# Expert loop: the down projection as three products of rounded halves, the second block's inner tile rounded later, both output copies on ScalarE

## What is computed

```
def moe_ffn(h, w_router, router_bias, w_e_gate, w_e_up, w_e_down, w_sh_gate, w_sh_up, w_sh_down):
    ...
    def expert_block(args):
        tok_b, w_b, e = args
        xb = h[tok_b]
        hid = jax.nn.silu(xb @ w_e_gate[e]) * (xb @ w_e_up[e])
        return (hid @ w_e_down[e]) * w_b[:, None].astype(h.dtype)
    out = lax.map(expert_block, (buf_tok.reshape(n_blocks, MOE_BLOCK), buf_w.reshape(n_blocks, MOE_BLOCK), block_e))
    routed = jax.ops.segment_sum(out.reshape(n_pad, d), buf_tok, num_segments=n_tok)
```

## Time and profile before

| | us |
|---|---|
| median of 3 runs | 3445.34 (3444.95 to 3451.27) |
| the profiled execution's own time | 3434.75 |
| its span, first to last instruction | 3432.9 |
| first product of the expert loop to the last (L2081 to L2096) | 987.3 to 1664.6 |

### The profile page before, as it was taken

One profiled execution on the slowest core, in us unless ns is written; L12 is line 12 of the kernel. 1 busy time (PEld: TensorE's weight loads), 2 busy tenths in 40 slices (PEclk: granted clock), 3 DMA queues, 4 the chain that ended last, 5 costly groups with the idle time before them and its releaser, 6 DMA issues.

```text
span 3432.9 us, 44220 instructions
## 1 busy us (share of the span) xinstructions
PE 3263.4 (95%) x16966; PEld 2567.5 (75%) x16966; DVE 1600.3 (47%) x2236; ACT 1448.6 (42%) x1847; POOL 1313.7 (38%) x1068
## 2 busy tenths in 40 slices
PE   7999998999889999999879999998999998899999
PEld 4788876778556666666567888887888877688887
DVE  4555437355476666666444554546221232452121
ACT  4344445612335555555444555555322242342221
POOL 2322136444123333333235434433444443354444
PEclk9999999999899999999989999999999999999999
DMA  5212110255259999999833222231322211022222
GB/s 212 68 50 62 38 50 13 87 184 196 76 219 344 349 344 357 377 366 367 311 108 104 89 84 83 81 101 60 110 99 90 99 58 62 25 98 98 98 98 74
DMA packets 98530, 496.85 MB, mean 145 GB/s; under 512 B 22446, under 2 KB 22702, under 8 KB 49728
## 3 DMA queue, kind: packets, MB, share of 16 engines
q1 hardware_dynamic: 78480, 454.86, 37.2%
q0 software_dynamic: 19888, 39.73, 3.2%
HBM read 472.48 MB, written 40.89 MB: 150 GB/s over the span
## 4 chain that ended last, share of the span: by engine, by line
PE 82%; DVE 5%; ACT 4%; DMA 3%; issue 3%; POOL 2%; SPq 0%; ACTq 0%; DVEq 0%; POOLq 0%
PE ps L283 13%; PE ps L285 13%; PE ps L284 13%; PE ps L2096 7%; PE ps L289 4%; PE ps L291 3%; PE ps L290 3%; PE ps L2081 3%; PE ps L2085 3%; PE ps L2084 3%; DMA arena<-we_gu 3%; PE ps L2634 1%; PE ps L2622 1%; PE ps L713 1%; PE ps L2070 1%
## 5 line engine op out<-in xcount | busy, mean ns | idle before, releaser
L283 PE MATMUL ps<-arena_r,arena_r 128*128 128x512 f32 x2080 | 823.9, 396 | 16.2 <-POOL ring_r L273 7.1
L284 PE MATMUL ps<-arena_r,arena_r 128*128 128x512 f32 x2080 | 813.0, 391 | 0.0
L273 POOL TENSOR_TENSOR ring_r<-ring,arena_r 128x512 fp32r<-128x512 f32 x400 | 553.0, 1413 | 644.4 <-ACT arena_r L268 644.4
L268 ACT ACTIVATE arena_r<-ring 128x2048 fp32r<-128x2048 f32 x166 | 316.8, 1910 | 407.2 <-PE ps L285 330.5
L273 POOL TENSOR_TENSOR arena_r<-ring,arena_r 128x512 fp32r<-128x512 f32 x264 | 335.1, 1301 | 381.1 <-ACT arena_r L268 381.1
L283 PEld LDWEIGHTS ps<-arena_r,arena_r 128*128 128x128 f32 x2080 | 392.6, 189 | 106.7 <-issue 18.1
L284 PEld LDWEIGHTS ps<-arena_r,arena_r 128*128 128x128 f32 x2080 | 392.8, 189 | 81.7 <-issue 1.9
L285 PE MATMUL ps<-arena_r,arena_r 128*128 128x512 f32 x1056 | 410.8, 389 | 0.0
L285 PE MATMUL ps<-arena_r,ring_r 128*128 128x512 f32 x1024 | 402.2, 393 | 0.0
L2184 DVE TENSOR_TENSOR arena_r<-arena,arena_r 128x2048 fp32r<-128x2048 f32 x132 | 301.8, 2288 | 166.1 <-ACT arena_r L2142 165.8
L2142 ACT ACTIVATE arena_r<-arena 128x2048 fp32r<-128x2048 f32 x132 | 250.9, 1910 | 125.5 <-DMA arena<-we_gu 102.7
(11 more groups left out here) (435 smaller groups left out, 5872.2 us busy)
## 6 DMA issues: line engine op xcount, KB each, us to landing
ring<-wstream SPq DMA_DIRECT2D x177, 1024.0 KB, 5.0
arena<-we_gu SPq DMA_DIRECT2D x132, 1024.0 KB, 8.0
arena<-we_down SPq DMA_DIRECT2D x66, 1024.0 KB, 7.3
arena<-arena SPq DMA_DIRECT2D x256, 64.0 KB, 2.0
arena<-ys SPq DMA_DIRECT2D x32, 512.0 KB, 7.1
arena<-wstream SPq DMA_DIRECT2D x24, 512.0 KB, 6.9
arena<-x_t SPq DMA_DIRECT2D x2, 2048.0 KB, 11.9
rope<-wstream SPq DMA_DIRECT2D x8, 512.0 KB, 8.5
```

The costliest lines, as they stand in the source:

```text
L268: act.activation(whalf(c, 0), ring[:, c % NSLOT, :], ACT.Copy).then_inc(sem("chunk_hi"), 1)
L273: ins = pool.tensor_tensor(whalf(c, 1)[:, q:q + 512], ring[:, c % NSLOT, q:q + 512], whalf(c, 0)[:, q:q + 512].bitcast(F32), ALU.subtract)
L283: pe.matmul(out, hi, rhs[0], start=start, stop=False)
L284: pe.matmul(out, hi, rhs[1], start=False, stop=False)
```

## The change

The down projection takes three products of rounded halves instead of one float32 product. For that, ScalarE gets a rounding of each block's down weights (`high_down`) and VectorE the subtraction (`low_down`), the turned inner tile of each block gets a high half by ScalarE (`hidden_high`) and a low half by VectorE (`hidden_low`) where before it had one copy, by ScalarE for block 0 and by VectorE for block 1. The new work for block 1 stands on ScalarE behind `turned(1)`, and on VectorE too. The copy of `YO[1]` goes from VectorE to ScalarE, and `high(1,1)` stands behind it. The load of `dmask_flat` is issued after the last pair, since the high half of block 1's down weights now uses its place.

```diff
             def down(s, j, first_done=None):
                 for k in range(2):
-                    mm = pe.matmul(bank(2 * s + j), HIDT[s][:, k * P:k * P + P], expert_raw(s, 2)[:, k * D + j * 512:k * D + j * 512 + 512],
-                                   start=(k == 0), stop=(k == 1))
+                    hidden = [half[:, k * P:k * P + P] for half in HIDT[s]]
+                    hi, lo = (w[:, k * D + j * 512:k * D + j * 512 + 512] for w in (expert_hi(s, 2), expert_lo(s, 2)))
+                    mm = pe.matmul(bank(2 * s + j), hidden[0], hi, start=(k == 0), stop=False)
...
+                    pe.matmul(bank(2 * s + j), hidden[0], lo, start=False, stop=False)
+                    mm = pe.matmul(bank(2 * s + j), hidden[1], hi, start=False, stop=(k == 1))
...
             def down_ready(i, s, back):
                 pe.wait_ge(sem(f"moe_hidt{s}"), i + (1 - back))
-                pe.wait_ge(sem(f"moe_w{s}2"), i * 16 + (16 - 16 * back))
+                pe.wait_ge(sem("moe_d_lo"), i * 2 + (s + 3 - 2 * back))
...
+            def high_down(s, i, back):
+                act.wait_ge(sem(f"moe_w{s}2"), i * 16 + (16 - 16 * back))
+                act.activation(expert_hi(s, 2), expert_raw(s, 2), ACT.Copy).then_inc(sem("moe_d_hi"), 1)
+
+            def hidden_high(s, i, back):
+                act.wait_ge(sem("moe_hturn"), i * 2 + (3 + s - 2 * back))
+                act.activation(HIDT[s][0], bank(6 + s, 256), ACT.Copy).then_inc(sem("moe_hidt_hi"), 1)
...
                 silu(i, 0, back)
+                high_down(0, i, back)
                 if not back:
                     turned(0, i + 2)
                     high(0, 0, i * 16 + 32)
                 silu(i, 1, back)
-                act.wait_ge(sem("moe_hturn"), i * 2 + (3 - 2 * back))
-                act.activation(HIDT[0], bank(6, 256), ACT.Copy).then_inc(sem("moe_hidt0"), 1)
+                hidden_high(0, i, back)
                 if not back:
                     turned(1, i + 2)
+                high_down(1, i, back)
+                hidden_high(1, i, back)
+                if not back:
                     high(0, 1, i * 16 + 32)
...
                 if not back:
-                    for j in range(2):
-                        high(1, j, i * 16 + 32)
+                    high(1, 0, i * 16 + 32)
+                act.wait_ge(sem("moe_d_used"), i * 2 + (4 - 2 * back))
+                act.wait_ge(sem("moe_out1"), i * 16 + (16 - 16 * back))
+                act.activation(YO[1], pf[:, 1024:2048], ACT.Copy).then_inc(sem("moe_y1"), 1)
+                act.activation(small[:, 61:62], epst[:, :], ACT.Copy).then_inc(sem("moe_y_full1"), 1)
+                if not back:
+                    high(1, 1, i * 16 + 32)
...
+            def low_down(s, i, back):
+                dve.wait_ge(sem("moe_d_hi"), i * 2 + (s + 3 - 2 * back))
+                dve.tensor_tensor(expert_lo(s, 2), expert_raw(s, 2), expert_hi(s, 2).bitcast(F32),
+                                  ALU.subtract).then_inc(sem("moe_d_lo"), 1)
+
+            def hidden_low(s, i, back):
+                dve.wait_ge(sem("moe_hidt_hi"), i * 2 + (s + 3 - 2 * back))
+                dve.tensor_tensor(HIDT[s][1], bank(6 + s, 256), HIDT[s][0].bitcast(F32),
+                                  ALU.subtract).then_inc(sem(f"moe_hidt{s}"), 1)
...
                 value(i, 0, back)
+                low_down(0, i, back)
                 if not back:
                     turned(0, i + 2)
                     low(0, 0, i * 4 + 5)
                 value(i, 1, back)
+                hidden_low(0, i, back)
                 if not back:
                     turned(1, i + 2)
-                dve.wait_ge(sem("moe_hturn"), i * 2 + (4 - 2 * back))
-                dve.tensor_copy(HIDT[1], bank(7, 256)).then_inc(sem("moe_hidt1"), 1)
+                low_down(1, i, back)
+                hidden_low(1, i, back)
                 if not back:
                     low(0, 1, i * 4 + 6)
                     low(1, 0, i * 4 + 7)
-                dve.wait_ge(sem("moe_d_used"), i * 2 + (4 - 2 * back))
-                dve.wait_ge(sem("moe_out1"), i * 16 + (16 - 16 * back))
-                dve.tensor_copy(YO[1], pf[:, 1024:2048]).then_inc(sem("moe_y1"), 1)
-                dve.tensor_copy(small[:, 61:62], epst[:, :]).then_inc(sem("moe_y_full1"), 1)
-                if not back:
                     low(1, 1, i * 4 + 8)
...
             pool.dma_start(rope[:, :, :], rope_t[1]).then_inc(sem("dil_loaded"), 16)
-            pool.dma_start(dmask_flat, dmask_t[:, 0:4 * TA]).then_inc(sem("dil_loaded"), 16)
             pool.dma_start(dmask_turned, dmask_t[:, 4 * TA:5 * TA]).then_inc(sem("dil_loaded"), 16)
             pool.dma_start(WZ, w_z).then_inc(sem("dil_loaded"), 16)
             pair_of_blocks(n - 1, False)
+            pool.dma_start(dmask_flat, dmask_t[:, 0:4 * TA]).then_inc(sem("dil_loaded"), 16)
```

More of the change, by code:

```diff
@@ L120 @@
                                        "moe_hidt", "moe_y", "moe_y_full") for s in "01") + (
-    "moe_gu_hi", "moe_gu_lo", "moe_gu_used", "moe_d_used", "moe_hturn", "moe_x_col", "moe_y_col")
+    "moe_gu_hi", "moe_gu_lo", "moe_gu_used", "moe_d_used", "moe_hturn", "moe_x_col", "moe_y_col",
+    "moe_d_hi", "moe_d_lo", "moe_hidt_hi")
 TAIL_SEMS = ("moe_left", "tl_act", "tl_weights", "tl_ranked", "tl_diag", "tl_turn", "tl_x", "tl_sq", "tl_xw", "tl_sum",
@@ L1742, in two_blocks @@
         XBT = [[rounded(4096 + 2048 * part + 1024 * s, D) for part in range(2)] for s in range(2)]
-        HIDT = [view(R + 30720 + 256 * s, 256) for s in range(2)]
+        HIDT = [[rounded(R + 30720 + 512 * s + 256 * part, 256) for part in range(2)] for s in range(2)]
         K0 = R + 31744
@@ L2167, in pair_of_blocks @@
                 if not back:
-                    for j in range(2):
-                        high(1, j, i * 16 + 32)
+                    high(1, 0, i * 16 + 32)
[5 more added lines that the diff above has]
+                    high(1, 1, i * 16 + 32)
             act.sem_inc(sem("moe_y0"), 1)
+            act.sem_inc(sem("moe_y1"), 1)
+            act.sem_inc(sem("moe_d_hi"), 2)
+            act.sem_inc(sem("moe_hidt_hi"), 2)
             for s in range(2):
@@ L2208, in pair_of_blocks @@
                     low(1, 0, i * 4 + 7)
-                dve.wait_ge(sem("moe_d_used"), i * 2 + (4 - 2 * back))
-                dve.wait_ge(sem("moe_out1"), i * 16 + (16 - 16 * back))
-                dve.tensor_copy(YO[1], pf[:, 1024:2048]).then_inc(sem("moe_y1"), 1)
-                dve.tensor_copy(small[:, 61:62], epst[:, :]).then_inc(sem("moe_y_full1"), 1)
-                if not back:
                     low(1, 1, i * 4 + 8)
-            dve.sem_inc(sem("moe_y1"), 1)
             dve.sem_inc(sem("moe_gu_lo"), 4)
+            dve.sem_inc(sem("moe_d_lo"), 2)
             for s in range(2):
```

## The result

| | before | after |
|---|---|---|
| median | 3445.14 us | 3522.3 us (3519.64 to 3525.92, 4 runs) |
| profiled execution, its span | 3434.75, 3432.9 | 3521.39, 3519.6 |
| mean granted clock | 0.979 | 0.968 |

What follows compares the result with a forecast made beforehand. TensorE looked like the bound, transfers close behind. 32 pairs at +1.24 us (+39.7), last pair -0.9 and the moved `dmask_flat` load 0.3 gave +39 on 3445.34: 3484 us, range 3467 to 3502.

Steps and rivals of the forecast that it cites:

- The chain: Expert loop, from `turned(1)` through `high_down(1)`, `low_down(1)`, `hidden_low(1)` to block 1's down products: pair becomes 21.65 us; 74%.
- TensorE's saving: Down products at 0.227 us each: 6.88 us a pair falls to 5.46, 1.42 us less if nobody waits.
- Copy of `YO[1]` free: Copy on ScalarE with `high(1,1)` behind: ready 5.5 to 6 us into the next pair, wanted 9 us in; no cost.
- I take most of it as gone, 0.1 us left per pair: Lateness of gate/up weights in the expert loop mostly vanishes in the longer pair: 0.1 us left, mean pair 21.75.
- the mean DMA share: Transfers in the expert loop, 19.5 us a pair: busy 0.90 of a 21.65 us pair instead of 0.95.
- The spare time: A late `high(0,0)` has 0.21 us to spare, then delays the pair one for one; 0.25 us before the change.
- The rival that kept the lateness: Lateness of weights in the loop stays or grows: +51, or +60 with another 0.3 us per pair, 3496 to 3505 us; 10%.
- The clock: Rival: clock drops to 1.2 GHz for the last 12 products of every pair, +79 us on top, 3563 us; 4%.
- one gap of 1.65 us that kept full clock: Evidence against the falling clock: from 2900 to 2920 TensorE is busy 16.82 of 20 us and keeps 2.4 GHz.
- a gap of 2.1 us ahead of `down(0,0)`: TensorE waits about 2.1 us in each pair as `down(0,0)` moves from 1516.16 to about 1518.30.
- The sum: 32 x 1.24 = +39.7 us for the loop's pairs, with the smaller terms +39 (bounds +35 and +53): median 3484 us.
- the last pair: Last pair of the expert loop, without next tokens to turn or such a chain: between -1.4 and 0, taken as -0.9 us.

Runs made afterwards that it cites:

- experiment 1: Changed kernel with the loop's scatters and gathers moving 64 of 1024 columns; pairs of 21.60 to 21.67 us, only the loop comparable.
- experiment 8: Changed kernel with block 1's down tile rounded before `silu(1)`, subtracted before `value(1)`, and tile (0,0) handled later; 3431.39 us.
- experiment 9: Changed kernel with block 1's down tile prepared early, `high(0,0)` directly behind `high_down(1)` and `hidden_low(0)` ahead of `value(1)`; 3429.12 us.
- experiment 6: Tile (0,0) rounded and subtracted later, behind the hidden tiles, in both kernels: 3430.16 us in the kernel before, 3512.97 us in the changed one.
- experiment 3: Changed kernel with the copy of `YO[1]` back on VectorE, behind `low(1,0)`; 3523.93 us.
- experiment 7: Useless products filling TensorE's idle time: 3518.85 us on the changed kernel, 3473.11 us on the changed kernel with tile (0,0) handled later.

## Why the prediction was wrong

- **The chain**: right. 21.65 forecast, 21.63 measured with nothing else in the way (experiment 1), each step of a short pair within 0.11 us, and experiment 8 removes it by order alone.
- **TensorE's saving**: right per product (one every 0.227 us). Of the 1.42 us a pair little was ever seen: the short pairs of experiment 9 are 0.2 us under those of experiment 6 in the kernel before, and TensorE still idles in them (busy 469.65 of 500 us).
- **Copy of `YO[1]` free**: right (experiment 3).
- **"I take most of it as gone, 0.1 us left per pair"**: this step failed. It was argued from the mean DMA share, which fell even further than the 0.90 forecast, to 0.85. What counts is when three loads in a row are asked for, and that is tied to the pair's end, not to its length. L was 10.80 before (by rows; 10.40 from the real start of the first product) and 10.66 after, so the longer pair did not bring the mean load in sooner. The spare time is as forecast (lengthening sets in at L = 10.0), but lateness now costs 0.91 us a pair, 29 us, instead of 0.1. The L of the kernel before, put into the formula of the changed one, give 0.44; the rest comes of the wider spread (8.63 to 12.85 after, 9.55 to 11.55 before). The rival that kept the lateness had 10%, and its 0.44 to 0.74 us a pair was too low as well.
- **The clock**: the rival was priced at 79 us and given 4%, because of one gap of 1.65 us that kept full clock. That row was right and proved too little: I forecast a gap of 2.1 us ahead of `down(0,0)` myself, longer than the one I held against the rival, and the late weights stretch it to up to 4.9 us. I put the clock at nothing in the sum and costed the two rivals apart, though the one makes the other. It cost 0.58 us a pair, 19 us, far from the rival's 79 too.
- **The sum**: 32 x (1.14 + 0.91 + 0.58) = 84 us, of 87 between the two profiled executions (77 between the medians: the profiled execution of before was 10 us under its median). With the load order mended the changed kernel takes 3480 us, which is what the forecast of 3484 described. By the traces the loop starts 1.9 us earlier, the 32 steps from pair to pair take 83.4 us more, the last pair 0.1 us less (0.9 forecast), and what lies behind the loop 5.3 us more; why was not tested. Nor was it found why the latest tiles came later than before (L up to 12.85, against 11.55 from the real start), except that scatters and gathers beside the loads are needed for it.

In the changed kernel of experiment 6 an idle stretch of 2.15 to 2.22 us in each pair, with one of some 0.35 us before it, goes with 3.4 us at 1.2 GHz in two pairs of three, and filling it ends that (experiment 7). That is what the Trainium skill (TensorE: Matmul & The Clock Gate, A second HAM failure mode) says of small idles between bursts; these runs agree with it, and I had let one row speak against it.

## What to carry to other kernels

A halved product doesn't help while its operand's preparation lies between two things that TensorE waits for: place the preparation first, then count the saving. In good order the change takes 3429 us, but moving one tile in the old kernel gives 3430, a difference within the runs' spread, so the edit with the better return is the smaller one. When a loop gets longer, look at what releases the request of each late load; a lower mean DMA share says nothing on a burst. And a wait that a change puts on TensorE has to be priced with the clock it may cost behind it: look for pairs with a gap as long as the one you expect, not for one that is shorter.

## What the hardware showed that I had not expected

- **Half clock behind idle time, 3.4 us at a time.** In the 341 pairs of the changed kernel and its ten variants none of 201 whose longest TensorE gap was under 1.9 us had a stretch at 1.2 GHz begin in it; of 51 with 1.9 to 2.2 us 30 had, of 29 between 2.2 and 3.3 us 18, and of 60 with 3.3 us or more 58. Even equal pairs differ (experiment 6: 20 stretches in 31 pairs, all with a gap of 2.15 to 2.22 us), so the gap alone does not decide.
- **GpSimd's indirect DMA instructions became longer, and the traces show what they wait for.** Issuing a gather took 1039 ns before and 2390 after, in the loop's stretch from 1100 to 1600 (before, then after); the gathers still came in time, since TensorE never idles ahead of a transpose.

```profile
L1794 POOL DMA_INDIRECT arena<-h,arena x50 | 51.9, 1039 | 44.0 <-POOLq L1793 40.5 <-issue 2.6 <-POOL arena L1791 0.9
```

```profile
L1795 POOL DMA_INDIRECT arena<-h,arena x43 | 102.8, 2390 | 37.9 <-POOLq L1794 37.9
```

Taken over 30 pairs of each of the 14 traces, 834 gathers and scatters were begun while a 128x2048 subtraction was already running on VectorE, and every one ended 0.87 to 0.94 us after that subtraction did. The 845 others took 0.99 to 1.07 us. In the kernel before none of 120 was begun so, in the changed one 93 of 120. Experiment 6 in the kernel before adds no work and only moves tile (0,0), and there block 0's scatter (L2238) falls into a subtraction (L2184) in 29 of 30 pairs and takes 2.3 to 2.6 us in them. GpSimd's and VectorE's timelines of it:

```profile
1233.39 2.52 POOL L2238 DMA_INDIRECT ys<-arena  x1 [0.89 <-POOLq L2237]
1232.72 2.29 DVE L2184 TENSOR_TENSOR arena_r<-arena,arena_r 128x2048 fp32r<-128x2048 f32 x1 [0.26 <-ACT arena_r L2142]
```

The same scatter in the kernel before, where the subtraction begins 0.5 us later than the scatter:

```profile
1214.61 1.02 POOL L2238 DMA_INDIRECT ys<-arena  x1 [0.89 <-POOLq L2237]
1215.13 2.29 DVE L2184 TENSOR_TENSOR arena_r<-arena,arena_r 128x2048 fp32r<-128x2048 f32 x1 [1.62 <-ACT arena_r L2142]
```

Whether this has a part in the late weights was not tested.
